# A hybrid encoder layer on one Trainium2 core: the softmax probabilities turned on VectorE and through scratch memory, and both weighted sums one block later

## What is computed

```python
qa, ka, va, qb, kb, vb, ga, gb = jnp.split(u @ w_in, cuts, axis=-1)
...
p = jax.nn.softmax(jnp.concatenate([logits, sink_l], axis=-1), axis=-1)[..., :-1]   # A: 8 query heads, 2 key/value heads, window
out = jnp.einsum('bnkgqs,bnskd->bnqkgd', p.astype(v.dtype), vb)
...
p = jax.nn.softmax(logits, axis=-1)                                                 # B: 8 heads, 2-D neighbourhood
out = jnp.einsum('bijhqk,bijkhd->bijqhd', p.astype(v.dtype), vg)
...
m = jax.nn.sigmoid(ga + bga) * (A @ w_up_a) + jax.nn.sigmoid(gb + bgb) * (B @ w_up_b)
return m @ w_out
```

## Time and profile before

| | |
|---|---|
| median of three runs | 2045.6 us |
| the profiled execution: time, span | 2045.57 us, 2043.8 us |
| TensorE busy | 2031.8 us, 99% of the span |
| VectorE, ScalarE, GpSimd busy | 1226.4 us, 1052.4 us, 50.0 us |
| granted TensorE clock, mean | 0.998 of full speed |
| DMA | 434.41 MB, mean 213 GB/s |

### The profile page before, as it was taken

How to read it: one execution, slowest core, us unless ns; L and a number is a source line. 1 busy time by engine, 2 the same in 40 slices (tenths; PEclk the granted TensorE clock), 3 DMA queues, 4 the chain that set the end, 5 groups by cost and what they waited for, 6 DMA issues and landing times.

```text
span 2043.8 us, 26721 instructions
## 1 busy us (share of the span) xinstructions
PE 2031.8 (99%) x9016; PEld 1680.8 (82%) x9016; DVE 1226.4 (60%) x1942; ACT 1052.4 (51%) x1845; POOL 50.0 (2%) x86
## 2 busy tenths in 40 slices
PE   9999999999999999999999999999999999999998
PEld 7888888888888888888888888888888888888887
DVE  6655555655555576666666676755555656555554
ACT  7545544555444564545555555565555555544443
POOL 1000000000000011110000000000000000000000
PEclk9999999999999999999999999999999999999999
DMA  8787777777556659886666586577777777775554
GB/s 300 219 229 228 215 220 219 222 226 243 194 195 196 203 183 260 248 250 185 176 184 176 190 248 214 177 217 213 214 215 214 222 223 213 215 235 193 193 194 144
DMA packets 248908, 434.41 MB, mean 213 GB/s; under 512 B 16504, under 2 KB 49272, under 8 KB 248448
## 3 DMA queue, kind: packets, MB, share of 16 engines
q1 hardware_dynamic: 244496, 421.61, 68.0%
q0 software_dynamic: 4336, 11.82, 2.8%
HBM read 412.65 MB, written 20.70 MB: 212 GB/s over the span
## 4 chain that ended last, share of the span: by engine, by line
PE 99%; DVE 1%; DMA 0%; ACT 0%; issue 0%; SPq 0%; DVEq 0%; ACTq 0%
PE acc L1049 32%; PE acc L1051 32%; PE acc L1050 32%; PE tp L1162 1%; PE tp L1185 1%; PE tp L1173 0%; PE tp L1087 0%; DMA raw<-in_ffn_w_in 0%; DVE WL L683 0%; DVE h L778 0%; DVE smax L922 0%; DVE V L880 0%; ACT WH L441 0%; PE tp L1125 0%; DVE fg L751 0%
## 5 line engine op out<-in xcount | busy, mean ns | idle before, releaser
L683 DVE TENSOR_TENSOR WL<-raw,WH 128x512 fp32r<-128x512 f32 x1424 | 970.9, 690 | 776.4 <-ACT WH L441 774.8
L441 ACT ACTIVATE WH<-raw 128x512 fp32r<-128x512 f32 x1424 | 890.9, 631 | 938.0 <-PE acc L1051 873.8
L1049 PE MATMUL acc<-WH,XH 128*128 128x512 f32 x2032 | 799.1, 393 | 2.8 <-DVE WL L683 2.8
L1051 PE MATMUL acc<-WH,XL 128*128 128x512 f32 x2032 | 791.9, 390 | 0.0
L1050 PE MATMUL acc<-WL,XH 128*128 128x512 f32 x2032 | 791.4, 389 | 0.0
L1049 PEld LDWEIGHTS acc<-WH,XH 128*128 128x128 f32 x2032 | 381.9, 188 | 82.1 <-issue 4.1
L1051 PEld LDWEIGHTS acc<-WH,XL 128*128 128x128 f32 x2032 | 381.9, 188 | 80.0
L1050 PEld LDWEIGHTS acc<-WL,XH 128*128 128x128 f32 x2032 | 382.0, 188 | 78.0
L1049 PE MATMUL acc<-WH,MH 128*128 128x512 f32 x688 | 267.6, 389 | 0.0
L1050 PE MATMUL acc<-WL,MH 128*128 128x512 f32 x688 | 267.6, 389 | 0.0
L1051 PE MATMUL acc<-WH,ML 128*128 128x512 f32 x688 | 267.6, 389 | 0.0
(11 more groups left out here) (109 smaller groups left out, 667.7 us busy)
## 6 DMA issues: line engine op xcount, KB each, us to landing
raw<-in_ffn_w_in SPq DMA_DIRECT2D x352, 512.0 KB, 4.5
raw<-in_ffn_w_out SPq DMA_DIRECT2D x176, 512.0 KB, 4.6
raw<-in_w_in SPq DMA_DIRECT2D x136, 512.0 KB, 4.5
raw<-in_w_out SPq DMA_DIRECT2D x32, 512.0 KB, 4.7
turned_blocks<-Z SPq DMA_DIRECT2D x29, 512.0 KB, 3.1
Y<-turned_blocks SPq DMA_DIRECT2D x116, 128.0 KB, 4.7
raw<-in_w_up_a SPq DMA_DIRECT2D x16, 512.0 KB, 5.1
raw<-in_w_up_b SPq DMA_DIRECT2D x16, 512.0 KB, 4.4
```

The lines of the kernel that those rows point to most:

```text
L441: act.activation(weight_hi(c), raw[:, c // 2 % RAW, c % 2, :], ACT.Copy).then_inc(hi_ready, 1)
L683: dve.tensor_tensor(weight_lo(c), raw[:, c // 2 % RAW, c % 2, :], weight_hi(c).bitcast(F32), ALU.subtract).then_inc(lo_ready, 1)
L1049: pe.matmul(a, hi[:, tok], weight_hi(c), start=first, stop=False)
L1051: return pe.matmul(a, lo[:, tok], weight_hi(c), start=False, stop=last)
```

## The change

The transposes on TensorE and ScalarE's copies of them are taken out. VectorE turns both heads of a block at once in 32 x 32 squares (`turn_probs`, behind its chunk 14) into the tile `Zprob`; SyncE stores that to scratch memory (`store_probs`) and fetches it into `Yprob` (`fetch_probs`), both within the loads of the next block. `prob_b` gets a place of its own. The weighted sums of both heads run together at chunk 3 of the next block (`both_values`), into banks 2 and 1; the moving operand is read from `Yprob` in runs of 32 elements. Their split into `YH` and `YL` is put behind ScalarE's chunk 12 and VectorE's chunk 15 of that block. For the last two heads it stands behind ScalarE's chunk 10 and VectorE's chunk 11 of the up-projection.

```diff
         EH, _ = place("EH", [P, WS, NB], F32R, o_m)
         EL, _ = place("EL", [P, WS, NB], F32R, o_m + FC * SEQ * 4)
-        prob = [place("prob_b", [P, TT, SEQ], F32, o_tmp)[0],
+        prob = [place("prob_b", [P, TT, SEQ], F32)[0],
                 place("prob_a", [P, TT, SEQ], F32, o_mask)[0]]
-        probT, _ = place("probT", [P, TT, SEQ], F32, o_tmp + TT * SEQ * 4)
+        Zprob, _ = place("Zprob", [P, 4 * TT * SEQ // 2], F32, o_tmp)
+        Yprob = [place("Yprob0", [P, 4, TT * SEQ // 2], F32, o_yl + 12288)[0],
+                 place("Yprob1", [P, 4, TT * SEQ // 2], F32, o_m)[0]]
+        pscr = nc.dram_tensor("turned_probs", [P * 2 * TT * SEQ], F32)
         rpad, _ = place("rpad", [B_H * RPB_USED, PADW], F32, o_yl)
...
         gainsT, _ = place("gainsT", [P, 3 * DC], F32, o_tmp)
...
             c, tiles = unit_tile(u)
             return x[:, c, tiles[0] * P:(tiles[-1] + 1) * P]
+        def prob_turned(n, kt):
+            return Yprob[n // 8][:, :, :].rearrange("p i (n t k s) -> p n k t i s", n=2, t=TT, k=TT)[:, n % 2, kt, :, :, :]
+        def y_bank(n):
+            return tp[:, 2 - n % 2, 0:SEQ]
         def sem(name):
             return ctx.enter_context(nc.semaphore(name))
...
                 for j in range(4):
...
                     sp.dma_start(y[32 * j:32 * j + 32, :, :].rearrange("p t (i f) -> p (t i) f", i=4), src).then_inc(blocks_landed, 16)
+            def store_probs(g):
+                sp.wait_ge(probs_turned, 2 * (g + 1))
+                if g:
+                    sp.wait_ge(probs_landed, 64 * g)
+                sp.dma_start(pscr[:].rearrange("(p f) -> p f", p=P), Zprob[:, :]).then_inc(probs_stored, 16)
+            def fetch_probs(g):
+                sp.wait_ge(probs_stored, 16 * (g + 1))
+                if g:
+                    sp.wait_ge(y_done, 2 * g)
+                row = 2 * TT * SEQ
+                for j in range(4):
+                    src = bass.AP(pscr, j * row // 4, [[row, 32], [32 * row, 4], [1, row // 4]])
+                    sp.dma_start(Yprob[g // 4][32 * j:32 * j + 32, :, :], src).then_inc(probs_landed, 16)
             def load(chunk, weights, chunks, col, more=0, units=None, di=0, at=0, z=Z, y=Y):
...
                 sp.dma_start(h[:, :, j * NB:(j + 1) * NB], x_tiles[:, :, j * NB:(j + 1) * NB]).then_inc(x_landed[j], 16)
...
             ffn(C_F1IN, C_F1OUT, W1I, W1O, Z_F1, DC + 4)
-            for b in range(QK_BLOCKS + GATE_BLOCKS):
+            for b in range(QK_BLOCKS + 1):
                 if 2 <= b < 2 + len(QK_HEADS):
...
                     load(C_QKV + b * DC, WIN, DC, b * NB)
-            for u in range(OUT_BLOCKS):
+            for g in range(1, GATE_BLOCKS):
+                chunk, col = C_GATE + g * DC, (QK_BLOCKS + g) * NB
+                load(chunk, WIN, 6, col)
+                store_probs(g - 1)
+                load(chunk + 6, WIN[6 * P:, :], 4, col)
+                fetch_probs(g - 1)
+                load(chunk + 10, WIN[10 * P:, :], 6, col)
+            load(C_UP, UPA, 6, 0)
+            store_probs(GATE_BLOCKS - 1)
+            load(C_UP + 6, UPA[6 * P:, :], 2, 0)
+            load(C_UP + 8, UPB, 2, 0)
+            fetch_probs(GATE_BLOCKS - 1)
+            load(C_UP + 10, UPB[2 * P:, :], 6, 0)
+            for u in range(1, OUT_BLOCKS):
                 if u < 2:
...
                 else:
...
                     act.activation(prob[n % 2][:, t, :], prob[n % 2][:, t, :], ACT.Exp, bias=nmax[:, n, t:t + 1],
                                    accum_out=psum_[:, n, t:t + 1]).then_inc(exp_ready, 1)
-            def copy_probT(n):
-                act.wait_ge(prob_turned, n + 1)
-                if n:
-                    act.wait_ge(y_done, n)
-                act.activation(probT[:, :, :], tp[:, 1, :].rearrange("p (a b) -> p a b", a=TT),
-                               ACT.Copy).then_inc(probT_ready, 1)
             def split_y_hi(n, hd, a):
                 act.wait_ge(y_done, n + 1)
-                act.activation(YH[:, hd, a, :], tp[:, 2, 0:SEQ], ACT.Copy).then_inc(y_hi, 1)
-            def finish_heads(c, g):
-                if c == 2:
-                    split_y_hi(2 * g, g, 1)
-                    copy_probT(2 * g + 1)
-                if c == 5:
-                    split_y_hi(2 * g + 1, g, 0)
+                act.activation(YH[:, hd, a, :], y_bank(n), ACT.Copy).then_inc(y_hi, 1)
             def sigmoids(u):
...
             for g in range(GATE_BLOCKS):
...
                     split_hi(C_GATE + g * DC + c)
-                    if g:
-                        finish_heads(c, g - 1)
                     if c == 9:
...
                         exps(2 * g + 1, g, True)
-                    if c == 15:
-                        copy_probT(2 * g)
+                    if g and c == 12:
+                        split_y_hi(2 * g - 2, g - 1, 1)
+                        split_y_hi(2 * g - 1, g - 1, 0)
             for u in range(OUT_BLOCKS):
...
                     split_hi(C_UP + u * 16 + c)
-                    if u == 0:
-                        finish_heads(c, A_Q - 1)
+                    if u == 0 and c == 10:
+                        split_y_hi(14, 7, 1)
+                        split_y_hi(15, 7, 0)
                     if c == 10:
...
                     if u >= 2 and c == 5:
...
                 for t in range(TT):
                     dve.tensor_scalar(prob[n % 2][:, t, :], prob[n % 2][:, t, :], rinv[:, n, t:t + 1], None, ALU.mult).then_inc(prob_ready, 1)
+            def turn_probs(g):
+                dve.wait_ge(prob_ready, 2 * TT * (g + 1))
+                if g:
+                    dve.wait_ge(probs_stored, 16 * g)
+                z = Zprob[:, :].rearrange("p (j n m s) -> p n m j s", j=4, n=2, m=2 * TT)
+                for n in range(2):
+                    dve.transpose(z[:, n, :, :, :], prob[n][:, :, :].rearrange("p t (k j s) -> p (t k) j s", k=TT, j=4)).then_inc(probs_turned, 1)
             def split_y_lo(n, hd, a):
                 dve.wait_ge(y_hi, n + 1)
-                dve.tensor_tensor(YL[:, hd, a, :], tp[:, 2, 0:SEQ], YH[:, hd, a, :].bitcast(F32),
+                dve.tensor_tensor(YL[:, hd, a, :], y_bank(n), YH[:, hd, a, :].bitcast(F32),
                                   ALU.subtract).then_inc(y_lo, 1)
             def mix_a(u):
...
                     split_lo(C_GATE + g * DC + c)
...
                         mask_bias(B_H - 1)
-                    if c == 2 and g:
-                        split_y_lo(2 * g - 2, g - 1, 1)
-                    if c == 5 and g:
-                        split_y_lo(2 * g - 1, g - 1, 0)
                     if c == 8:
...
                     if c == 9:
...
                         read_gate(g - 1)
...
                         probabilities(2 * g + 1, g, True)
+                    if c == 14:
+                        turn_probs(g)
+                    if c == 15 and g:
+                        split_y_lo(2 * g - 2, g - 1, 1)
+                        split_y_lo(2 * g - 1, g - 1, 0)
             for u in range(OUT_BLOCKS):
...
                     split_lo(C_UP + u * 16 + c)
-                    if u == 0 and c == 2:
+                    if u == 0 and c == 11:
                         split_y_lo(14, 7, 1)
-                    if u == 0 and c == 5:
                         split_y_lo(15, 7, 0)
...
                         read_gate(GATE_BLOCKS - 1)
...
                                    start=True, stop=True)
                 mm.then_inc(scores_done, 1)
-            def turn_prob(n):
-                pe.wait_ge(prob_ready, TT * (n + 1))
-                if n:
-                    pe.wait_ge(probT_ready, n)
-                for kt in range(TT):
-                    for t in range(TT):
-                        o = kt * SEQ + t * P
-                        tr = pe.transpose(tp[:, 1, o:o + P], prob[n % 2][:, t, kt * P:(kt + 1) * P], ident[:, :])
-                tr.then_inc(prob_turned, 1)
             def weighted_values(n, v0):
...
                         pe.wait_ge(acc_freed[b % 2], freed_before(b) + TT)
-                pe.wait_ge(probT_ready, n + 1)
-                if n:
-                    pe.wait_ge(y_lo, n)
+                pe.wait_ge(probs_landed, 64 * (n // 2 + 1))
+                if n >= 2:
+                    pe.wait_ge(y_lo, n - 1)
                 for kt in range(TT):
-                    mm = pe.matmul(tp[:, 2, 0:SEQ], V[:, kt, v0:v0 + HD], probT[:, kt, :], start=kt == 0, stop=kt == TT - 1)
+                    mm = pe.matmul(y_bank(n), V[:, kt, v0:v0 + HD], prob_turned(n, kt), start=kt == 0, stop=kt == TT - 1)
                 mm.then_inc(y_done, 1)
+            def both_values(g):
+                weighted_values(2 * g, (A_KV + g) * HD)
+                weighted_values(2 * g + 1, g // 4 * HD)
             pe.wait_ge(ident_ready, 2)
             for k in range(WARM):
...
                     if c == 0:
...
                         scores(2 * g + 1, g, 8 + g // 4, 3)
-                    if c == 7:
-                        turn_prob(2 * g)
```

(20 more changed lines are left out.)

## The result

| | before | changed |
|---|---|---|
| median | 2045.6 us | 2037.63 us (2036.59 to 2037.97, 5 runs) |
| ratio | | 0.9958, 95% interval 0.9948 to 0.9969 |
| profiled execution: span | 2043.8 us | 2035.2 us |
| TensorE, VectorE, ScalarE busy | 2031.8, 1226.4, 1052.4 us | 2022.8, 1235.9, 1045.8 us |
| DMA | 434.41 MB | 442.81 MB |

The changed kernel is 8.0 us faster by the medians and 8.6 by the spans; 2037.0 was forecast. Lines of the new kernel are numbered anew: the chunk matmuls are L1081 to L1083, the scores L1194, the sums L1207, the turns L969, the splits of the sums L637 and L973.

What follows compares the result with a forecast made beforehand. TensorE was taken to bound the kernel, busy for all 26.37 us of a gate block. Gains of 8.8 and 0.5 us less a 0.7 us wait made 8.6: from 2045.57 to 2037.0 us, range 2035.8 to 2040.0.

Steps and rivals of the forecast that it cites:

- What is removed: TensorE in gate blocks: transposes gone and sums run together save 1.10 us a block, 8.8 us over eight blocks.
- The rival that spoke of "no wait in a gate block but that of block 0": Gate blocks: the transposes are not off the path, something else takes their 8 us; about 2045 us, chance 2%.
- Block 0: First gate block: its transposes' wait for the probabilities goes too, 0.5 us gained beyond the other blocks.
- VectorE: Gate blocks: two turns of 0.69 us and two splits of 0.4 are added, covered by slack, so no cost.
- that cover: Slack of 8 us before TensorE wants chunk 16's low half; without it VectorE's added work costs 2 us a block.
- One sign: VectorE in a gate block: turns at 0.69 us each, ending ahead of 16 us after the block's scores start.
- S: The moment at which a gate block's scores start on TensorE; the forecast counts turns, store, fetches and sums from it.
- The queue: SyncE's queue in gate blocks: one 512 KB store and four fetches added a block, 4.4 us of slack, no cost.
- The wait: Up-projection, chunk 7: TensorE waits 0.60 us for the last YL and loses 0.7 us, once; this case had 70%.
- R: The moment at which chunk 3 of the up-projection would start, where the last two sums now run.
- Runs of 32 elements: Weighted sums on TensorE: reading the moving operand in such runs was taken to cost nothing; high end 13.8 us.
- The doubling of the rival: Weighted sums: reading 32-element runs takes twice the time, 13.8 us more, 2050.8 us; chance 6%, half of it in between.

## Why the prediction was right

Start to start, from the scores of block 0 to chunk 7 of the up-projection, the kernel before takes 221.03 us (927.67 to 1148.70) and the changed one 212.05 (928.00 to 1140.05): 8.98 us gained, where 8.6 were forecast. Of the difference 0.2 is a block that is shorter by 1.13 and not 1.10, and 0.1 a wait that is shorter. The spans show 8.6 because the profiled start was 0.33 us slower in the changed kernel (below). The medians show 8.0; their spread is 1 us and more, and I take it for the same, without having shown it.

- **What is removed.** The size was right. 0.45 and 0.55 us for the two transposes were worth 1.13 us a block with the fewer pieces; 1.10 was forecast. One step was wrong: that ScalarE's copies go was put at nothing, "since it idles for half a block". The copy held PSUM bank 1, and 0.10 us a block of what I called the price of the transposes was a wait for it. It lay inside the measured distance, so the sum did not suffer. The rival that spoke of "no wait in a gate block but that of block 0" rested on the same misreading.
- **Block 0.** 26.87 less 23.50 less the 1.74 of its sums leaves 1.63, so 0.50 more than the 1.13 of the others, as forecast.
- **VectorE.** The turns took 0.70 and 0.67 us and made no chunk late. No run took that cover away. One sign failed: they should end ahead of S + 16 and end at S + 16.8. The forecast took the place of chunk 14 from the kernel before, where no sums stand at chunk 3. In the changed kernel the high half of chunk 11 waits until TensorE has finished chunk 3, behind the sums; before, ScalarE did not wait there:

```profile
985.86 0.63 ACT L481 ACTIVATE WH<-raw 128x512 fp32r<-128x512 f32 x1 [1.23 <-PE acc L1083]
```

The low half of chunk 14 then starts at S + 14.9 (991.67 - 976.74) and not at S + 13.7.
- **The queue.** That it costs nothing was right; the room was worked out too wide, and two of the errors cancel by luck. Forecast: the store out at S + 15.7, landed after 4.6; fetches landed at S + 26.7, room 4.4. Measured in block 2: the store out at S + 16.9 (993.60 - 976.74), 1.2 later, and landed after 2.9, 1.7 sooner. The 4.6 was a median of stores and fetches together, with four fetches to each store; the page of the kernel before has 3.1 for its stores alone. For the fetches the forecast took the median too, where the last of the four counts: it landed 6.3 us behind the start of its issue, at S + 27.5, and the room was 3.6 us. In the up-projection no scores stand ahead of the sums, so they come at S + 29.3 (1132.26 - 1102.94) and not at S + 31.1, and the room was 1.2 us. The forecast did not look at that place. The two runs with later fetches show that beyond the room a late landing is paid in full, and more than that behind an idle time of 3.6 us, where the granted clock fell to 0.53 and 0.71.
- **The wait.** Forecast from the durations on ScalarE and VectorE: YL done at R + 7.80, chunk 7 at R + 7.20 without it, 0.7 us lost. Measured: R + 7.73, R + 7.18 and 0.61. The run with YL earlier shows the cause.
- **Runs of 32 elements.** Taken at nothing, measured at nothing. The doubling of the rival exists, at 16 bytes between elements.
- **The rule on transposes** (the Trainium skill, VectorE: DVE Perf Modes, section Rules for kernel authors) names TensorE for a 128x128 turn if the result may go to PSUM. In this kernel TensorE is the one engine without room. So its eight turns of a block, 0.97 us by the run that put them back, were dearer than turns of 1.4 us on VectorE, a store of 2.9 and fetches of 4.2 to 7.7, all of them hidden.

The price of one later block for the sums was a new place in two other engines' lists. There 0.61 us were lost of what the change gained, and one line gave them back.

## What to carry to other kernels

Where one engine is busy for the whole stretch, price each of its small jobs by starts: the distance between the matmuls around it, less the ordinary steps. Then ask which of them can go by a longer way that ends before its reader comes; the length of the way is free as long as it fits, and is paid in full beyond that. Reckon the room from the transfer that lands last, and for each place where the reader stands: here it was 3.6 us in one block and 1.2 us in the up-projection. When a job moves, follow what stands ahead of it on every engine's list, since a short split behind a table load came late though its input was long there.

## What was not expected of the hardware

The start, whose work is the same in all these kernels, took up to 1.25 us more in one profiled execution than in another (scores of block 0 at 927.51 in the run with YL earlier, at 928.76 in that with the sums later). TensorE's timeline, last slow matmul, of the kernel before and of the run with the sums later:

```profile
12.04 0.56 PE L1051 MATMUL acc<-WH,XL 128*128 128x512 f32 x1
```

```profile
13.59 0.56 PE L1054 MATMUL acc<-WL,XH 128*128 128x512 f32 x1
```

Ahead of it, from 9.05 and from 8.47, matmuls show 0.63 us instead of 0.39, which is the lower clock; the kernel before had run its first ones at 0.40. At the 17th chunk matmul one kernel is 1.09 us behind the other (14.46 against 13.37), and it still is at the scores of block 0. Where a fraction of a microsecond is in question, distances inside the trace tell it and medians do not.

The wait of 1.08 us of TensorE (the fetches two loads later) left the sums behind it at 1.99 us; the wait of 3.65 us in the same run brought them to 3.66. The wait of 3.58 us (three loads later) brought them to 2.76 and the next stretches to a granted clock of 0.71 and 0.81.

Matmuls behind a short float32 piece take steps of 0.231 us in place of 0.227 for ten or so. Why is open; it makes up 0.04 us of the 0.49 for four transposes.
